# The V projection of a decoder trunk: products 512 columns wide, a third place for split weights, weight blocks in another order

## The reference, cut to what matters

```python
def rms_norm(x, g, eps=RMS_EPS):
    xf = x.astype(jnp.float32)
    y = xf * lax.rsqrt(jnp.mean(xf * xf, axis=-1, keepdims=True) + eps)
    return (y * g.astype(jnp.float32)).astype(x.dtype)

def differential_attention(h, w_in, lam_qk, subln_g, w_out, rel_table, lambda_init):
    B, S, D = h.shape                       # 1, 2048, 1024
    proj = h @ w_in
    q, k, v = jnp.split(proj, [D, 2 * D], axis=-1)
    v = v.reshape(B, S, DIFF_HEADS, DIFF_V_DIM).transpose(0, 2, 1, 3)   # 8 heads of 128
    ...
```

## Time and profile before

| | us |
|---|---|
| median of three runs | 2729.49 (2728.29 to 2731.19) |
| the profiled execution | 2731.74 |
| its span, first to last instruction | 2730.2 |
| mean granted TensorE clock in it | 0.919 of full speed |
| Q and K fills begin / V fills begin | 67.45 / 416.04 |
| last V fill's last eight matmuls begin | 599.39 |
| first load of `attend` issued / its first matmul | 603.39 / 624.74 |

### The profile page before, as it was taken

The page is one execution under the profiler, slowest core; times in us unless marked ns, Lnnn a source line. Parts: engine busy times, 40 slices in busy tenths (PEclk is TensorE's granted clock), DMA queues, the critical chain, the costliest instruction groups (busy, mean ns, idle before and its releaser), DMA issues. The chain is left out here.

```text
span 2730.2 us, 36997 instructions
## 1 busy us (share of the span) xinstructions
PE 2355.8 (86%) x11480; PEld 1886.0 (69%) x11480; DVE 1419.9 (52%) x2813; ACT 1187.0 (43%) x1605; POOL 664.9 (24%) x464
## 2 busy tenths in 40 slices
PE   5999999976999999999869994769999999999920
PEld 3888889974666666666558884657888887887710
DVE  6221211005666766666346664656656556566646
ACT  5111111114666666666532221455645555555523
POOL 0000000004666666666400111100101111111133
PEclk7999999996999999999979996889999999999965
DMA  5333334124543554353145331677776876886768
GB/s 178 136 111 130 121 118 116 47 66 109 132 119 99 133 131 125 101 135 92 51 144 185 123 115 50 250 270 296 269 279 224 297 270 230 303 311 255 269 238 307
DMA packets 228007, 473.62 MB, mean 173 GB/s; under 512 B 20073, under 2 KB 72465, under 8 KB 225874
## 3 DMA queue, kind: packets, MB, share of 16 engines
q1 hardware_dynamic: 203026, 391.00, 42.4%
q0 software_dynamic: 17072, 53.79, 5.8%
q10 hardware_dynamic: 7824, 27.79, 2.9%
HBM read 355.30 MB, written 117.21 MB: 173 GB/s over the span
## 5 line engine op out<-in xcount | busy, mean ns | idle before, releaser
L1325 DVE TENSOR_TENSOR gu_lo<-gu_raw,gu_hi 128x2048 fp32r<-128x2048 f32 x128 | 293.3, 2291 | 160.0 <-ACT gu_hi L1256 117.5
L585 DVE TENSOR_SCALAR_CACHE_REDUCE p_ring<-ps_s 128x256 f32<-128x256 f32 (+7 forms) x352 | 277.6, 792 | 157.9 <-PE ps_s L656 151.4
L522 POOL TENSOR_TENSOR p_ring<-p_ring 128x1152 f32<-128x1152 f32 (+15 forms) x128 | 321.7, 2513 | 10.7
L550 ACT ACTIVATE p_ring<-p_ring,shift 128x1152 f32<-128x1152 f32 (+15 forms) x256 | 305.9, 1197 | 27.1 <-DVE shift L601 27.1
L1256 ACT ACTIVATE gu_hi<-gu_raw 128x2048 fp32r<-128x2048 f32 x128 | 239.0, 1909 | 178.1 <-DMA gu_raw<-in_moe_w_up 102.0
L691 PE MATMUL ps_o<-aT,v_st 128*128 128x512 f32 (+3 forms) x640 | 291.9, 540 | 0.0
L539 ACT ACTIVATE aT<-ps_t 128x512 f32<-128x512 f32 (+1 forms) x320 | 168.1, 531 | 227.2 <-PE ps_t L676 227.1
L656 PE MATMUL ps_s<-k,q_st 128*128 128x512 f32 (+3 forms) x640 | 209.1, 454 | 43.7 <-DMA near<-near_rows 24.2
L1417 PE MATMUL ps_g<-gu_hi,xT_lo 128*128 128x512 f32 x720 | 236.4, 410 | 4.3 <-DVE xT_lo L1340 3.6
L1417 PE MATMUL ps_g<-gu_lo,xT_hi 128*128 128x512 f32 x720 | 231.8, 403 | 0.0
L1417 PE MATMUL ps_g<-gu_hi,xT_hi 128*128 128x512 f32 x720 | 231.0, 402 | 0.0
(11 more groups left out here) (223 smaller groups left out, 4220.3 us busy)
## 6 DMA issues: line engine op xcount, KB each, us to landing
gu_raw<-in_moe_w_gate SPq DMA_DIRECT2D x128, 512.0 KB, 7.9
gu_raw<-in_moe_w_up SPq DMA_DIRECT2D x128, 512.0 KB, 8.9
d_raw<-in_moe_w_down SPq DMA_DIRECT2D x64, 1024.0 KB, 5.0
qk<-stage SPq DMA_DIRECT2D x64, 512.0 KB, 2.8
q_st<-qk SPq DMA_DIRECT2D x128, 256.0 KB, 5.1
y_rows<-y_sb ACTq DMA_DIRECT2D x45, 512.0 KB, 3.3
y_rows<-nil SPq DMA_DIRECT2D x32, 512.0 KB, 6.2
w_raw<-in_diff_w_in POOLq DMA_DIRECT2D x12, 1024.0 KB, 6.7
```

Source lines behind the costliest of these rows:

```text
L522: pool.tensor_tensor(p0(r, 0, w), p0(r, 0, w), p1(r, 0, w), ALU.add).then_inc(mixed, 1)
L550: nc.scalar.activation(p, p, ACT.Exp, bias=shift[:, r % 8, m:m + 1], accum_out=sums[:, r % 8, m:m + 1]).then_inc(raised, 1)
L585: ins = nc.vector.tensor_scalar(p(r, k0, k0 + far), ps_s[:, c % 2, 0:far], SCALE, None, ALU.mult, ALU.max, accum_out=top[:, r % 4, m, col: ...
L1325: nc.vector.tensor_tensor(gu_lo[:, j * GC:(j + 1) * GC], gu_raw[:, j], gu_hi[:, j * GC:(j + 1) * GC].bitcast(F32), ALU.subtract).then_inc( ...
```

## The change

The two pairs of split places `w_hi`, `w_lo` become one tensor `w3` with three places of 16 KB per partition, each with its hi and lo half (`w_place` only reserves the memory of the first two; the third is the memory of `xt` and `k0`). The order in which blocks are loaded and split is now `ORDER`, with the place in `SLOT` and the fill that frees the place in `FREED`. Block 9 comes after block 4, is split in the middle of block 3's fills into the third place, and lies there until it is used. Its split also waits for what was in the x buffer (`turned`, `moved`). Block 11 comes before block 10.

V is now made in two passes of 16 fills, each of 24 matmuls with 512 columns: the first takes blocks 8 and 9 from places 0 and 2, the second blocks 10 and 11 from places 0 and 1. A matmul's streamed operand is then two pieces of 256 columns out of two places. Place 0 is free for block 10 only when the first pass is through, so the first two tiles of the second pass are made in halves: first block 11's 256 columns of tiles 0 and 1, then block 10's. ACT copies 512 columns, and the stores are of 256 KB. The load of `k0` moves from before the first pass to before the second one's stores, with a wait for the first pass's last fill. The loops of DVE, POOL and SP over blocks are written out; PE's loop over Q and K blocks becomes two, and from block 4 on it waits for one more split.

```diff
-        w_hi = sb("w_hi", [P, 2, KC, WB], F32R)
-        w_lo = sb("w_lo", [P, 2, KC, WB], F32R)
+        ctx.enter_context(nc.sbuf_tensor("w_place", [P, 2, 2, KC, WB], F32R, side="right"))
+        w3 = keep["w3"]
...
-        V_FILLS = VB * TILES
+        V_FILLS = VB // 2 * TILES
+        ORDER = (0, 1, 2, 3, 4, 9, 5, 6, 7, 8, 11, 10)
+        SLOT = (0, 1, 0, 1, 0, 2, 1, 0, 1, 0, 1, 0)
+        FREED = (None, None, 8, 16, 24, None, 32, 40, 48, 56, QK_FILLS, QK_FILLS + TILES)
...
-            with sp.Fori(0, VB) as b:
+            for b in range(VB // 2):
+                if b == 1:
+                    for i in range(4):
+                        sp.wait_ge(stored[i], 16 * QK_FILLS // 4 + 1)
+                    sp.wait_ge(filled, QK_FILLS + TILES + 1)
+                    for hl in range(2):
+                        sp.dma_start(k0[hl * HALF:(hl + 1) * HALF].bitcast(F32),
...
-                    nc.scalar.activation(stage[:, n % 4, 0:WB].bitcast(F32), ps[:, n % 8, 0:WB], ACT.Copy).then_inc(out_lo, 1)
+                    nc.scalar.activation(stage[:, n % 4, 0:512].bitcast(F32), ps[:, n % 8, :], ACT.Copy).then_inc(out_lo, 1)
...
-            for b in range(VB):
-                if b + 1 < VB:
-                    split(QKB + b + 1, (b + 1) % 2, QK_FILLS + b * TILES)
+            for b in range(QKB):
+                split(ORDER.index(b + 1))
+                for n in range(8):
+                    if b == 3 and n == 4:
+                        split(ORDER.index(9))
+                    take(b * 8 + n + 1, stage[:, n % 4, 512:1024], stage[:, n % 4, 0:512], ps[:, n, :])
+            split(ORDER.index(11))
+            split(ORDER.index(10))
...
+            for first, loads in ((0, 2), (2, 3)):
+                with pe.Fori(first, first + 2) as b2:
+                    for half in range(2):
+                        pe.wait_ge(w_split, b2 * 2 + (half + loads))
...
+            def fill_v(n, slots, c0, c1):
+                k = 0
+                for w, h in ((LO, hnT_hi), (HI, hnT_lo), (HI, hnT_hi)):
+                    for c in range(KC):
+                        mm = pe.matmul(ps[:, n % 8, c0:c1], h[:, c, n * P:(n + 1) * P], w3[:, slots, w, c, :],
+                                       start=k == 0, stop=k == 23)
+                        k += 1
+                return mm
+
+            pe.wait_ge(w_split, ORDER.index(8) + 2)
+            for n in range(TILES):
+                pe.wait_ge(out_lo, QK_FILLS + n + 1)
+                fill_v(n, slice(0, 3, 2), 0, 512).then_inc(filled, 1)
+            pe.wait_ge(w_split, ORDER.index(11) + 2)
+            for n in range(2):
+                pe.wait_ge(out_lo, QK_FILLS + TILES + n + 1)
+                fill_v(n, 1, WB, 512)
+            pe.wait_ge(w_split, ORDER.index(10) + 2)
+            for n in range(2):
+                fill_v(n, 0, 0, WB).then_inc(filled, 1)
+            for n in range(2, TILES):
+                pe.wait_ge(out_lo, QK_FILLS + TILES + n + 1)
+                fill_v(n, slice(0, 2), 0, 512).then_inc(filled, 1)
```

More of the change, by code:

```diff
@@ L147, in _ @@
                                pattern=[[1, P]], channel_multiplier=1).then_inc(flip_set, 1)
-            with pool.Fori(0, BLOCKS) as b:
-                gate(pool, w_split, b + 1, passed)
-                pool.dma_start(w_raw[:, :, :], w_rows[:, :, bass.ds(b * WB, WB)]).then_inc(w_in, 16)
+            for at, b in enumerate(ORDER):
+                gate(pool, w_split, at + 1, passed)
+                pool.dma_start(w_raw[:, :, :], w_rows[:, :, b * WB:(b + 1) * WB]).then_inc(w_in, 16)
         @block.scalar
@@ L191, in _ @@
             act.wait_ge(out_lo, BANKS + QK_FILLS)
-            with act.Fori(0, VB) as b:
+            with act.Fori(0, VB // 2) as b:
                 for n in range(TILES):
@@ L225, in scale, with split @@
                                                in1=g_row[:, :], op0=ALU.mult, op1=ALU.mult).then_inc(normed, 1)
-            def split(b, slot, freed=None):
-                dve.wait_ge(w_in, b * 16 + 16)
-                if freed is not None:
-                    dve.wait_ge(filled, freed + 1)
-                nc.vector.tensor_copy(w_hi[:, slot], w_raw[:, :, :]).then_inc(w_hi_set, 1)
-                dve.wait_ge(w_hi_set, b + 1)
-                nc.vector.tensor_tensor(w_lo[:, slot], w_raw[:, :, :], w_hi[:, slot].bitcast(F32),
+            def split(at):
+                dve.wait_ge(w_in, at * 16 + 16)
+                if FREED[at] is not None:
+                    dve.wait_ge(filled, FREED[at] + 1)
+                if SLOT[at] == 2:
+                    dve.wait_ge(turned, 12 + TURNED0)
+                    dve.wait_ge(moved, 32)
+                nc.vector.tensor_copy(w3[:, SLOT[at], HI], w_raw[:, :, :]).then_inc(w_hi_set, 1)
+                dve.wait_ge(w_hi_set, at + 1)
+                nc.vector.tensor_tensor(w3[:, SLOT[at], LO], w_raw[:, :, :], w3[:, SLOT[at], HI].bitcast(F32),
                                         ALU.subtract).then_inc(w_split, 1)
@@ L239, in take @@
                 nc.vector.tensor_tensor(dst, src, hi.bitcast(F32), ALU.subtract).then_inc(out_lo, 1)
-            split(0, 0)
+            split(0)
             scale(0)
@@ L252, in _ @@
                 nc.vector.tensor_copy(unskewed[:, k * 512:(k + 1) * 512], ps[:, (2, 3, 6, 7)[k], :]).then_inc(z_set, 1)
-            with dve.Fori(0, QKB // 2) as b2:
-                for half in range(2):
-                    split(b2 * 2 + half + 1, 1 - half, b2 * 16 + half * 8)
-                    for n in range(8):
-                        take(b2 * 16 + half * 8 + n + 1, stage[:, n % 4, 512:1024], stage[:, n % 4, 0:512], ps[:, n, :])
-            for b in range(VB):
-                if b + 1 < VB:
-                    split(QKB + b + 1, (b + 1) % 2, QK_FILLS + b * TILES)
+            for b in range(QKB):
[6 more added lines that the diff above has]
+            split(ORDER.index(10))
         @block.tensor
@@ L290, in _ @@
             pe.wait_ge(hn_lo, TILES + 2)
-            with pe.Fori(0, QKB // 2) as b2:
-                for half in range(2):
-                    pe.wait_ge(w_split, b2 * 2 + (half + 2))
-                    for n in range(8):
-                        if half == 0 and n == 2:
-                            pe.wait_ge(z_set, 7)
-                        pe.wait_ge(out_lo, b2 * 16 + (half * 8 + n + 1))
-                        k = 0
-                        for w, h in TERMS:
-                            for c in range(KC):
-                                mm = pe.matmul(ps[:, n, :], w[:, half, c, (n // 4) * P:(n // 4 + 1) * P],
-                                               h[:, c, (n % 4) * 512:(n % 4 + 1) * 512], start=k == 0, stop=k == 23)
-                                k += 1
-                        mm.then_inc(filled, 1)
@@ new lines, in _ @@
+            for first, loads in ((0, 2), (2, 3)):
+                with pe.Fori(first, first + 2) as b2:
+                    for half in range(2):
+                        pe.wait_ge(w_split, b2 * 2 + (half + loads))
+                        for n in range(8):
+                            if half == 0 and n == 2:
+                                pe.wait_ge(z_set, 7)
+                            pe.wait_ge(out_lo, b2 * 16 + (half * 8 + n + 1))
+                            fill_qk(half, n)
+            def fill_v(n, slots, c0, c1):
+                k = 0
+                for w, h in ((LO, hnT_hi), (HI, hnT_lo), (HI, hnT_hi)):
+                    for c in range(KC):
+                        mm = pe.matmul(ps[:, n % 8, c0:c1], h[:, c, n * P:(n + 1) * P], w3[:, slots, w, c, :],
+                                       start=k == 0, stop=k == 23)
+                        k += 1
+                return mm
@@ L1616, in build @@
             keep["xt"] = xt
+        with nc.sbuf_tensor("w3", [P, 3, 2, KC, D // 4], F32R, side="right") as w3:
+            keep["w3"] = w3
         k0 = ctx.enter_context(ExitStack())
```

29 lines of the change are left out of this document (8 added, 21 removed).

## The result

The changed kernel takes 2742.28 us (median of 6 runs, 2738.27 to 2746.25), the kernel before, run beside it, 2730.34 (2726.36 to 2732.41). The ratio of the runs is 1.0048, 95% interval 1.0037 to 1.0058 (of the two medians alone 1.0044). The forecast was 2720.4, with 0.03 on slower.

What follows compares the result with a forecast made beforehand. PE alone was taken to bound the Q, K and V fills. V's -9.6 us and the tail's +0.5 gave -9.1, so 2729.49 became 2720.4 us; range 2717.5 to 2727, 8 times in 10.

Steps and rivals of the forecast that it cites:

- The pace of the wide matmuls: Q and K fills: 226.7 ns per 512-column matmul, measured in the kernel before and used for V's wide matmuls.
- The V fills: In project: 184.3 us falls to 174.7 with 720 wide and 96 narrow matmuls, a saving of 9.6 us.
- The two pieces: V's wide matmuls: streaming an operand from two places costs nothing extra; bounds among near rows 0 to 13.3 ns each.
- A: Rival, 720 wide V matmuls: the second piece costs as much as its own matmul; 2730.0 us, no change; chance 0.10.
- B: Rival, V fills: the 13.3 ns aren't per matmul where input tiles are loaded; wide takes 240.0 ns, total 2730.0; chance 0.03.
- C: Rival, 720 wide V matmuls: the jump empties the pipeline, 162 ns each, 117 us; total 2837 us; chance 0.03.
- The 2.5 ns per matmul: The skill's gap per matmul at the high clock, making the V term 1.8 us; the prediction used the trace's 13.3 ns.
- The tail: End of project after the last fill: longer copy +0.2 us and larger store +0.3 us, together +0.5 us.
- Block 9: Its split moves to the middle of block 3's fills, done 16.7 us before PE needs it; nothing is delayed.
- the seam: Between V's passes: block 10's split takes 3.8 us, covered by 5.8 us of narrow matmuls, 1.9 us to spare.
- k0: Its load, issued at about 503 us, lands by 520, needed near 615; delayed stores cost PE nothing.
- From there all is as before: From attend's first matmul on, everything runs as in the kernel before, only 9.1 us earlier.

Runs made afterwards that it cites:

- e2: Kernel before with w_hi and w_lo 32 bytes further up, all else unmoved: 2733.64 us, ratio 1.0013 to the kernel before.
- e5: Changed kernel with w3 moved down 96 bytes to 180096, a multiple of 256 from hnT: 2728.49 us, ratio 0.9984 to the kernel before.
- e6: Kernel before with hnT and the projection weights all 32 bytes higher, distances kept: 2729.66 us, ratio 1.0000 to the kernel before.
- e7: Kernel before with 43 idle wait instructions more on VectorE at the end of project: 2737.15 us, ratio 1.0017 to the kernel before.
- the padded kernels: Changed kernel with w3 at 180096 and 83 to 85 more VectorE instructions, some with further pads: attend 767.3 to 768.7 us in seven traces.
- e1: Changed kernel with the three weight places moved down 32 bytes, k0 unmoved: 2737.70 us, ratio 1.0025 to the kernel before.
- e4: Changed kernel with 32 bytes free at the top, so w3, xt and k0 begin at multiples of 64: 2737.68 us, ratio 1.0032 to the kernel before.
- e8: Kernel before with 418 idle wait instructions more on TensorE at the start of project: 2765.27 us, ratio 1.0122 to the kernel before.

## Why the prediction was wrong, by its own steps

- **The pace of the wide matmuls, carried over to a moved operand**, is the step that failed first. The sum had no term at all for Q and K, whose weights the change moves, and its `720 x 0.2267` took their pace over for V. Q's and K's went from 226.7 to 234.3 ns, 1536 x 7.6 ns = 11.7 us, for the weights' place alone (e2, e5, e6).
- **The V fills** have 720 wide and 96 narrow matmuls, as said. The narrow ones have the forecast 120.0 ns, the wide ones 233.3 instead of 226.7, for the same reason: from 427.41 to 605.07 + 8 x 0.2333 it is 179.5 us, a saving of 4.8 instead of 9.6. The working was right but for that number. With the distance put back (e5) V takes 174.7 us, the very number of the working.
- **The two pieces** cost nothing: in e5 wide V matmuls come at the same 226.7 ns as Q's and K's. That settles rivals A, B and C: none was true. The slow pace of the changed kernel lies halfway to A's 240.0, and it would have been easy to take it for half of A; e2, where no operand has two pieces, says no. The 2.5 ns per matmul that the prediction took from the Trainium skill (TensorE: Matmul & The Clock Gate, Back-to-back issue gap) are given there for a matmul by itself, not for a stream with weight loads between; e5's stream again shows 13.3, with its 226.7 and 120.0.
- **The tail** was to grow by 0.5 us. From the last copy's start to `attend` it was 603.39 - 600.55 = 2.84 before and is 610.52 - 607.13 = 3.39: +0.55.
- **Block 9, the seam, `k0`**: right. PE has no gap; the subtraction at the seam ends at 520.83, where 5.8 us of cover from 517.0 last until 522.77, with the forecast 1.9 us to spare.
- **"From there all is as before"** failed too, and this is the larger part in the profiled execution, +11.7 us. The text passed over the written-out loops with one sentence, on how fast they are fetched. Their cost did not lie where they run. They moved VectorE's pauses in the next stage (e7: +7.4 us in the profiled execution with the same 41.0 us at 1.2 GHz at the start, +0.17% in time). Of the 11.7 us the position accounts for 2 to 5 by the padded kernels and the longer start at 1.2 GHz, which kernels with the old position have too, for 1 to 5; the rest stays open.
- The sum by these steps: Q and K +11.7, V -4.8, tail +0.55: +7.45, and `project` is 7.5 us longer. `attend` adds 11.7, the rest takes 4.7: +14.5, the difference of the spans.

The rows to doubt the first step with stood in the trace of before: the experts' wide matmuls came 233 ns apart while Q's and K's came at 226.7, in one kernel, at one clock. A pace that differs between two places of the same shape has a cause, and a change that moves an operand can move it. A rival with 1536 + 720 matmuls at 233 ns would have read: 2729.49 + 2256 x 0.0066 - 9.1 = 2735.3, slower by 0.2%.

## What to carry to other kernels

Before counting on the measured pace of a matmul, write down where its two operands lie: here 512-column fp32 matmuls ran at 226.7 ns with a distance that is a multiple of 256 bytes and at 229 to 234 at the three other distances tried, so a tile that is moved changes every instruction that reads it (and a pad of 224 bytes in another stage, 0.36%, gained more than the rearrangement with its distance put back, 0.16%). And where a stage behind the edit got longer with the same instructions, compare instruction by instruction for pauses that moved, not only the code for edits; and compare it with more than one trace of the kernel before, since with VectorE's pauses at their old places, within one, the old kernel's attention stage took anything from 760.4 to 765.0 us.

## What the runs showed of the hardware that I had not expected

- The pace of matmuls by the distance of the operands, modulo 256 bytes: 0: 226.7 ns for 512 columns, 120.0 for 256; 32 (e2): 233.3 and 116.7; 64 (e1, e4): 233.3 with weights loaded, 229 with weights streamed; 96 (the changed kernel): 234.3 and 233.3. A distance of 128 was not tried, and no run says what in the chip does it.
- VectorE pauses for 0.35 us at fixed places of its order, some 256 recorded instructions apart from one another in one series (333, 589, 845), and a second series lies between (458, 715, 972). The Trainium skill (Advanced Engine Details and Errata, ISA Cache) says that instructions are cached in lines of 256; the spacing agrees. That the pauses are the fetching of such a line is likely by that and was not shown.
- A pause that moves by seven instructions, with the same work done, goes with another number of falls to 1.2 GHz: 16 stretches in e7 where the kernel before has 13. The gap on PE that grows with it, from 1.63 to 2.00 us, is followed by half speed in the changed kernel and by full speed in e7.
- The stretch at 1.2 GHz with which the attention stage begins is 41.0 us or 54.6 to 64.9 us long, in kernels that differ by a pad alone (41.0 in the kernel before, 58.0 in e2). What sets its length was not found.
- Waits that need not wait cost TensorE 79 ns per instruction (e8).
